# Attention by query blocks on quarters of the matmul array, with other stages' work placed between its steps

## The reference, cut to what matters

```python
h_c = modulate(rms_norm(ctx, g_norm_mix[layer]), csh_m, csc_m)
kc, vc = jnp.split(h_c @ w_in_l[:, Q_W:V_END], 2, axis=-1)
h_x = modulate(rms_norm(x, g_norm_mix[layer]), sh_m, sc_m)
qx, kx, vx, fx, glx = split_in_proj(h_x @ w_in_l)
qx = apply_rope(rms_norm(to_heads(qx, N_HEADS), g_q[layer]), cos, sin)
kx = apply_rope(rms_norm(to_heads(kx, N_KV_HEADS), g_k[layer]), cos, sin)
attn_x = blocked_attention(qx, k_all, v_all)   # softmax over 256 context + 2048 latent keys
g_attn, g_four = jnp.split(jax.nn.sigmoid(gate_logits + b_gate), N_BRANCH, axis=-1)
merged = g_attn * (attn @ w_attn_proj) + g_four * (fourier_mix(four) @ w_fourier_proj)
x = x + gt_m * (merged @ w_o)
x = x + gt_f * swiglu(modulate(rms_norm(x, g_norm_ffn[layer]), sh_f, sc_f), w_gate_up[layer], w_down[layer])
return rms_norm(x, g_final)
```

## Time and profile before

| | us |
|---|---|
| median of 3 runs | 1676.18 (1675.09 to 1676.6) |
| profiled execution, device time | 1671.44 |
| its span, slowest core | 1670.1 |
| PE busy, share | 1439.7, 86% |
| ACT busy, share | 925.3, 55% |
| DVE busy, share | 741.0, 44% |
| spans of the eight cores | 1653.5 to 1670.1 |

### The profile page before, as it was taken

How to read it: one execution, slowest core, us unless ns; L and a number is a source line. 1 busy time by engine, 2 the same in 40 slices (tenths; PEclk the granted TensorE clock), 3 DMA queues, 4 the chain that set the end, 5 groups by cost and what they waited for, 6 DMA issues and landing times.

```text
span 1670.1 us, 24822 instructions; the slowest of 8 cores (1653.5 to 1670.1 us)
## 1 busy us (share of the span) xinstructions
PE 1439.7 (86%) x7012; PEld 551.1 (33%) x7012; DVE 741.0 (44%) x994; ACT 925.3 (55%) x1470; POOL 36.4 (2%) x51
## 2 busy tenths in 40 slices
PE   0476668999999999999989999457899999999997
PEld 0232233222222222222334444213344444444443
DVE  3177779646555555555553333124311111212344
ACT  2587773999999999999922222017921111112111
POOL 1000000000000000000010000100000000000000
PEclk9999999999999999999999999679999999999999
DMA  9911100000000000000471130795682122202232
GB/s 191 158 38 39 51 14 1 1 1 1 14 1 1 14 1 1 14 1 1 54 98 22 24 45 1 142 168 182 173 168 48 29 40 37 51 26 76 107 116 81
DMA packets 48551, 93.16 MB, mean 56 GB/s; under 512 B 3233, under 2 KB 34082, under 8 KB 46754
## 3 DMA queue, kind: packets, MB, share of 16 engines
q0 software_dynamic: 34160, 43.52, 17.6%
q1 hardware_dynamic: 14258, 48.06, 8.6%
HBM read 118.31 MB, written 16.78 MB: 81 GB/s over the span
## 4 chain that ended last, share of the span: by engine, by line
PE 73%; DVE 8%; DMA 6%; ACT 6%; issue 5%; DVEq 0%; POOL 0%; ACTq 0%; POOLq 0%; another core or an unknown queue 0%
PE PS L353 73%; DMA SB<-w_ada 6%; ACT SB L377 6%; DVE SB L381 5%; DVE SB L411 2%; DMA SB<-w_in 1%; DVE SB L420 1%; PE PS L357 0%; DVE SB L405 0%; DVEq L254 0%; ACT SB L410 0%; POOL SB L262 0%; ACTq L254 0%; ACT L377 0%
## 5 line engine op out<-in xcount | busy, mean ns | idle before, releaser
L353 PE MATMUL PS<-SB 128*128 128x512 bf16 (+4 forms) x6540 | 1411.4, 375 | 171.7 <-DMA SB<-w_ada 67.5
L353 PEld LDWEIGHTS PS<-SB 128*128 128x128 bf16 (+1 forms) x6540 | 520.7, 98 | 1038.8 <-issue 614.6
L377 ACT ACTIVATE SB<-PS 128x1024 bf16<-128x1024 f32 (+2 forms) x714 | 607.3, 1003 | 258.3 <-PE PS L353 255.9
L381 DVE TENSOR_TENSOR SB<-PS,SB 128x512 f32<-128x512 f32 (+4 forms) x290 | 184.4, 664 | 579.6 <-PE PS L353 545.3
L377 ACT ACTIVATE SB<-SB 128x8 f32<-128x8 f32 (+3 forms) x285 | 145.8, 512 | 222.4 <-DVE SB L381 196.6
L381 DVE TENSOR_TENSOR SB<-SB 128x128 bf16<-128x128 f32 (+8 forms) x464 | 237.7, 531 | 46.9 <-DMA SB<-x 11.2
L377 ACT ACTIVATE SB<-PS,SB 128x128 bf16<-128x128 bf16 (+1 forms) x336 | 145.9, 531 | 184.8 <-PE PS L353 141.7
L417 DVE RECIPROCAL SB<-SB 64x512 f32<-64x512 f32 x64 | 214.2, 3347 | 4.2
L411 DVE COPY SB<-PS 128x1024 f32<-128x1024 f32 (+1 forms) x40 | 44.5, 1116 | 225.0 <-PE PS L353 224.8
L357 PE MATMUL PS<-SB 128*128 128x128 bf16 x472 | 40.7, 230 | 49.2 <-ACT SB L377 29.8
L410 ACT COPY SB<-PS 128x512 bf16<-128x512 bf16 (+2 forms) x50 | 35.5, 720 | 47.7 <-PE PS L353 23.7
(11 more groups left out here) (10 smaller groups left out, 11.7 us busy)
## 6 DMA issues: line engine op xcount, KB each, us to landing
SB<-x SPq DMA_DIRECT2D x32, 512.0 KB, 4.5
SB<-w_ada POOLq DMA_DIRECT2D x12, 1024.0 KB, 19.9
SB<-w_gu POOLq DMA_DIRECT2D x11, 1024.0 KB, 8.7
x_scratch<-SB SPq DMA_DIRECT2D x16, 512.0 KB, 5.3
SB<-x_scratch SPq DMA_DIRECT2D x16, 512.0 KB, 3.4
out<-SB SPq DMA_DIRECT2D x16, 512.0 KB, 2.6
SB<-w_dn POOLq DMA_DIRECT2D x2, 2816.0 KB, 32.6
SB<-w_in POOLq DMA_DIRECT2D x4, 1024.0 KB, 60.6
```

Of the source, the lines that this page charges most:

```text
L353: return K.op("pe", lambda h: h.matmul(out.ap, lhsT=lhsT.ap, rhs=rhs.ap, start=start, stop=stop), reads=[lhsT, rhs], writes=[out], cost=12 ...
L377: return K.op("act", lambda h: h.activation(out=out.ap, in_=in_.ap, func=func, **kw), reads=reads, writes=writes, cost=ecost("act", in_))
L381: return K.op(eng, lambda h: h.tensor_tensor(out=out.ap, in0=a.ap, in1=b.ap, op=op), reads=[a, b], writes=[out], cost=(1600.0 if op == ALU ...
```

## The change

The change rewrites the plan and the layout of nearly all stages.

- All weights are packed on the host so that each partition's part is contiguous (w_ada in 12 pieces of 16 KB a partition, w_in split into w_q, w_kv, w_f, and w_mix, which joins the gate, attention and Fourier projection columns of two column blocks). The columns of w_q and the rows of w_ap are permuted by heads.
- Phase A makes keys and values for 18 tiles (context last) and queries for the first block of 512 tokens alone. `P1` copies the transposed tile out of PSUM unmodulated in one ACT copy; `MOD` modulates two tiles at a time on DVE in place, bf16, eight tensor_scalar operations. The key is not doubled any more, and keys of two heads lie on the two halves of the partitions.
- Attention runs query block by query block (4 blocks, 8 units each). Key-query and value products each use four matmuls with 64x64 weights, one on each quarter of the array. The softmax sum is formed from bf16 additions of the probability tiles on DVE (13 additions of 128x1024 a unit) and then ten 512-column matmuls with a ones matrix; at the end of a unit DVE adds the two halves of the numerator and takes reciprocals in four pieces of 128. Scores have two pairs of banks; six buffers hold the probabilities; banks 6 and 7 are for other work.
- Between the steps, queries of the next block, the Fourier projection, its DFTs, the late modulation, and the merge groups of the first token block are placed, metered by a credit of 1.6 atoms a step (an atom is about one 512-column matmul). Gates use Tanh of half the argument in place of Sigmoid, with the factor one half put into the gate GTm.
- After attention, the merge of token blocks 1 to 3 (and what is left of block 0), with w_o and the first tiles of x loaded during it. In E1 the modulation is on DVE and the reciprocal root is two POOL operations, as in the final norm.
- The planner goes by the recorded order, with three lower classes of priority for filler matmuls, has a price for changing between the full and the quartered array, and latencies by engine.

```diff
+    LAT = {"pe": 390.0, "act": 190.0, "dve": 190.0, "pool": 300.0, "sp": 100.0}
+    LOW = 1 << 20
+    MIX = 1 << 21
+    LAST = 1 << 22
+    SWITCH_NS = 105.0
+    AHEAD_NS = 130.0
...
-                    heapq.heappush(rh, (-nd.bl, i, nd))
+                    heapq.heappush(rh, (nd.prio, i, nd))
...
+            if e == "pe":
+                top = run_h[e][0][2] if from_run else wait_h[e][0][2]
+                if top.prio >= self.LOW:
+                    soon = [it for it in wait_h[e][:40] if it[2].prio < self.LOW and it[0] <= st + self.AHEAD_NS]
+                    if soon:
+                        it = min(soon)
+                        wait_h[e].remove(it)
+                        heapq.heapify(wait_h[e])
+                        st, _, n = it
...
+            if e == "pe" and n.mode != pe_mode:
+                pe_mode = n.mode
+                st += self.SWITCH_NS
...
-    wada_d = din("w_ada", [D, 6 * D])
+    wada_d = din("w_ada", [12, 128, 4096])
...
+    wmix_d = din("w_mix", [4, 128, 7168])
...
+    ada_seq = ((1, 0), (1, 1), (0, 0), (0, 1))
+    for i in range(4):
+        ada_load(ada_slots[i], (0, 1)[ada_seq[i][0]], ada_seq[i][1])
+    loadw(Wkv, wkv_d.rearrange("p (k n) -> p k n", k=8))
+    for i in range(4):
...
+    def rstd(dst, ms, n=1):
+        ts("pool", dst, ms, EPS, ALU.add)
+        tt("pool", dst, dst, sub(mhalf, mhalf.ap[:, 0:n]), ALU.pow)
...
+        cp("act", dst, sub(pT, pT.ap.rearrange("p (k t) -> p k t", k=8)), outs=outs)
+
+    def MOD(t):
+        for k in range(8):
+            if t < NT:
+                o = (t // 4) * 4096 + k * 512 + (t % 4) * 128
+                v = rng(hT, hT.ap[:, t // 4, k, (t % 4) * 128:(t % 4) * 128 + 256], o, o + 256, 2)
+                m = 0
+            else:
+                v = rng(hcT, hcT.ap[:, k, :], k * 256, k * 256 + 256, 2)
+                m = 2
+            ts("dve", v, v, rng(modc, modc.ap[:, m, k:k + 1], m * 8 + k, m * 8 + k + 1, 4), ALU.mult,
+               rng(modc, modc.ap[:, m + 1, k:k + 1], m * 8 + 8 + k, m * 8 + 9 + k, 4), ALU.add, per=0.27)
+
...
+        act(sq, pv, AF.Square, scale=0.125)
+        tt("dve", h3(u), h3(pv), sub(tabv, tab(0).unsqueeze(1).to_broadcast([128, nh, 64])), ALU.mult)
+        tt("dve", h3(w), h3(pv), sub(tabv, tab(1).unsqueeze(1).to_broadcast([128, nh, 64])), ALU.mult)
+        reduce_sum(ss, h3(sq))
+        rstd_act(rs, ss, nh)
+        tt("dve", h4(u), h4(u), swapped(w, nh), ALU.add)
+        tt("dve", h3(outb), h3(u), sub(rs, rs.ap.unsqueeze(2).to_broadcast([128, nh, 64])), ALU.mult)
...
+    def Q_groups(qb):
+        for hf in range(2):
+            for tl in range(4):
+                if qb == 2:
+                    add_group(1, 10, late_ada.pop(0), 286)
+                    add_group(1, 0, ada_prefetch, 286)
+                add_group(max(qb - 1, 0), 9, lambda t=qb * 4 + tl, hf=hf: Qhalf(t, hf), 144 * qb - 2)
+
+    late_ada = [lambda vi=vi, hf=hf: ada_late_cols(vi, hf) for vi in (2, 3) for hf in range(2)]
+    late_ada += [lambda gt=gt, v=v, hf=hf: ada_late_rows(gt, v, hf) for gt, v in ((GTm, 2), (GTf, 5)) for hf in range(2)]
+    N0, N1 = 144 + 16, 432
+    add_group(0, 0, load_f, N0)
+    Q_groups(1)
+    for fg in range(4):
         for tb in range(4):
...
-            act(gsl[0], pGa, AF.Sigmoid, bias=sub(bgate, bgate.ap[:, j:j + 1]))
...
+    def give(qb, n):
+        credit[0] += n
+        while groups and credit[0] > 0 and groups[0][0] <= qb:
+            emit_group()
+        credit[0] = min(credit[0], 4.0)
...
+    def qk(n):
+        qb, c, kt = steps[n]
+        p = c // 4
+        b0 = (n % 2) * 2
+        parts = []
+        for kc in range(2):
+            for h in range(2):
+                o = p * NKT * 128 + kt * 128 + kc * 64
+                l_ = rng(kT, kT.ap[h * 64:(h + 1) * 64, p, kt * 128 + kc * 64:kt * 128 + kc * 64 + 64], o, o + 64, 2)
+                r_ = rng(qT, qT.ap[h * 64:(h + 1) * 64, qb, c, :], qb * 4096 + c * 512, qb * 4096 + c * 512 + 512, 2)
+                lo = (b0 + h) * 2048
+                o_ = View(PS[kc * 64:kc * 64 + 64, (b0 + h) * 512:(b0 + h + 1) * 512], "ps", lo, lo + 2048)
+                parts.append((o_, l_, r_, True, True))
+        mms(parts, mode=1, cost=216.0)
+
+    def av(n):
+        qb, c, kt = steps[n]
+        pt = PTs[n % NPT]
+        p = c // 4
+        parts = []
+        for r in range(2):
+            for h in range(2):
+                hd = 2 * p + h
+                l_ = rng(V, V.ap[r * 64:(r + 1) * 64, kt, hd * 64:hd * 64 + 64], kt * 256, kt * 256 + 256, 2)
+                parts.append((half(4 + r, h), l_, sub(pt, pt.ap[r * 64:(r + 1) * 64, h * 512:(h + 1) * 512]),
+                              kt == 0, kt == NKT - 1))
+        mms(parts, mode=1, cost=216.0)
+
...
+            tt("dve", slot, a, b, ALU.add, per=0.52)
+        else:
+            slot = cur["sums"][-1]
+            tt("dve", ptmp, a, b, ALU.add, per=0.52)
+            tt("dve", slot, slot, ptmp, ALU.add, per=0.52)
...
+        cp("dve", xs, bank(4), late=-30)
+        tt("dve", xs, xs, bank(5), ALU.add, late=-30)
+        ss = cur["sums"]
+        b = next_bank()
+        K.level = 1
+        for i, s_ in enumerate(ss):
+            for h in range(2):
+                mm(bank(b), sub(ones, ones.ap[:, h, :]), sub(s_, s_.ap[:, h * 512:(h + 1) * 512]),
+                   i == 0 and h == 0, i == len(ss) - 1 and h == 1)
+        K.level = 0
+        cp("dve", rd, bank(b))
+        at = attnTs[qb]
+        L = 60
+        for hh in range(4):
+            v = rng(rd, rd.ap[:, hh * 128:(hh + 1) * 128], hh * 128, hh * 128 + 128, 4)
+            recip(v, v, late=L)
+        tt("dve", rng(at, at.ap[:, c, :], c * 512, c * 512 + 512, 2), xs, rd, ALU.mult, late=L)
+        credit[0] -= 10
...
+    def step(n):
+        qb, c, kt = steps[n]
+        pt = PTs[n % NPT]
+        act(pt, s_bank(n), AF.Exp)
+        if n + 2 < len(steps):
+            qk(n + 2)
+        if kt % 2 == 1:
+            av(n - 1)
+            av(n)
+            pair_add(n)
...
+    RATE = 1.6
+    for t in range(4):
+        P1(t)
+    MOD(0)
+    MOD(2)
+    for t in range(4):
+        KV(t)
+        Qhalf(t, 0)
+    for t in range(4, NKT, 2):
+        P1(t)
+        P1(t + 1)
+        MOD(t)
+        KV(t)
+        KV(t + 1)
+    for t in range(4):
+        Qhalf(t, 1)
+    qk(0)
+    qk(1)
+    bank_set[0] = [6, 7]
+    for n in range(len(steps)):
+        qb, c, kt = steps[n]
+        drain(n)
+        step(n)
+        if kt == NKT - 1:
+            finish_unit(qb, c)
+        give(qb, RATE)
+    K.level = 3
...
+            act(tF if part else tA, bank(b), AF.Tanh, scale=0.5, bias=rng(bgate, bgate.ap[:, jb:jb + 1], jb, jb + 1, 4))
+        elif part == 1:
+            group(b, 8, lhs, lambda k: at_v(tb, k))
+            stt("dve", tA, tA, 1.0, bank(b), ALU.add, ALU.mult)
+        else:
```

More of the change, by code:

```diff
@@ L53, in __init__ @@
         self.tk = None
-        self.bl = 0.0
+        self.prio = 0
+        self.mode = 0
 class _Rec:
@@ new lines, in mms, with fn @@
+    def mms(parts, mode=0, cost=None):
+        def fn(h):
+            for o_, l_, r_, st_, sp_ in parts:
+                ins = h.matmul(o_.ap, lhsT=l_.ap, rhs=r_.ap, start=st_, stop=sp_)
+            return ins
+        if cost is None:
+            cost = sum(max(30.0, 2.0 + 0.418 * fsz(p[2])) for p in parts)
+        reads, seen = [], set()
+        for p in parts:
+            for v in (p[1], p[2]):
+                if (v.sp, v.lo, v.hi) not in seen:
+                    seen.add((v.sp, v.lo, v.hi))
+                    reads.append(v)
+        writes, seen = [], set()
+        for p in parts:
+            if (p[0].lo, p[0].hi) not in seen:
+                seen.add((p[0].lo, p[0].hi))
+                writes.append(p[0])
+        return K.op("pe", fn, reads=reads, writes=writes, cost=cost, mode=mode)
@@ new lines, in half, with group, trs, fn @@
+    def half(b, h):
+        lo = b * 2048
+        return View(PS[h * 64:(h + 1) * 64, b * 512:(b + 1) * 512], "ps", lo, lo + 2048)
+    def group(b, nk, lhs, rhs, more=False):
+        for k in range(nk):
+            mm(bank(b), lhs(k), rhs(k), k == 0, k == nk - 1 and not more)
+    def trs(pairs, ident):
+        def fn(h):
+            for o_, i_ in pairs:
+                ins = h.transpose(out=o_.ap, in_=i_.ap, identity=ident.ap)
+            return ins
+        return K.op("pe", fn, reads=[p[1] for p in pairs] + [ident], writes=[p[0] for p in pairs], cost=64.0 * len(pairs))
@@ L362, in act @@
+    def act(out, in_, func, scale=1.0, bias=None, accum=None, late=0):
+        reads = flat([in_])
         kw = {}
@@ L481, in build @@
     load(gcols, gcols_d)
+    load(ident, ident_d)
     load(gq_bc, gq_d.partition_broadcast(128))
```

1075 lines of the change are left out of this document (528 added, 547 removed).

## The result

The changed kernel takes 1595.35 us (median; 1594.25 to 1596.59), 0.952 of the time before, interval 0.950 to 0.954. It is 81 us faster; the prediction said 176, and 1595 is above its range too. The direction was right and the size was not.

A forecast was written before the change was run, and what follows sets the result against it. Outside attention, merge and feed-forward PE was half idle; that work moves into attention, bound by DVE. 1670.1 - 7.5 - 125.4 + 108.4 - 32.8 - 31.6 - 88.3 = 1492.9, 1500 us to be measured, range 1440 to 1590.

The forecast's parts named there:

- DVE's sum: Attention: all DVE work adds to 623 us, 1.08 a step, so DVE becomes the bound, just over PE and ACT.
- land at about 43 instead of 50, and four tiles are normalised meanwhile: Start-up: early w_ada pieces land sooner beside x and the key table; modc at 47.5 instead of 55, -7.5 us.
- I add 4% to the highest: Attention: four limits between 1.0 and 1.08 a step and a fixed order give 1.12 a step, 645 us.
- Rival 2: Attention: the two-bank chain and wrong planner costs make 1.3 a step, 749 us, total 1604; chance 0.13.
- The chain of two banks: Attention: Exp n, key-query group n+2, Exp n+2 take 0.87 us a step, or 1.03 with one filler and mode change.
- 144 steps x 1.6 - 8 x 10 = 150 atoms: Attention and merge: block 0 merge matmuls fitting into attention by credit, 32 us, leaving (896 - 150) x 0.216 = 161 us.
- the w_gu and w_down loads stand behind those roots: E1, POOL's queue: these loads follow the roots but have a whole pair's time in hand; no cost counted.
- the price of the modulation: E1: eight small DVE operations at 0.12 us a tile, within DVE's 3.7; the stage taken at 4.4 a tile, 70 us.
- rivals 3 and 4: Attention: column halves run serially, total 1707 us, chance 0.04; or bf16 additions take 1.22 us, total 1749, chance 0.02.
- The warning that queued fillers could hold the freeing of the sums: Attention: a sign that would prove the prediction wrong, queued fillers delaying the freeing of the sums; no size given.
- The changes of array mode: Attention, PE: two or three changes between full and quartered array a step at 0.10 us, 115 to 170 us.
- the second way of rival 3: Attention: quarters' weight loads stand before each group, 0.4 us a group, 1.79 a step, total above 1850; chance 0.02.

The follow-up runs named there:

- ada_split4: Each w_ada piece loaded by four instructions with 2 KB packets instead of 8 KB, against the changed kernel: 1582.57 us, ratio 0.946 to the kernel before.
- half_adds: Eight of the 13 softmax-sum additions of each unit left out, against the changed kernel: 1594.76 us in one execution.
- rate185: Filler credit of 1.85 atoms a step in place of 1.6, against the changed kernel: 1591.84 us, 0.9505 of the kernel before.
- one_wait: Only the last wait of each semaphore kept instead of one for each predecessor, against the changed kernel: 1573.35 us, 0.940 of the kernel before.
- e1_mod_act: Two of eight E1 modulations a tile moved from DVE to ACT, against the changed kernel with single waits, split w_ada loads and look-ahead off: 1529.37 us, for 1532.48.

## Why the prediction was wrong, point by point

In the attention the mechanism failed: it was put at DVE's sum and 4%, and that sum doesn't bind. In the start-up and in E1 a wait was put at nothing (x beside large packets, 15 us; the roots behind queued waits, 18 us), and in the merge a term was too small by 17. The four misses make 112 us; the span is over by 102, as two stages came out 10 below.

- **Start-up (+23.6).** The step that failed is "land at about 43 instead of 50, and four tiles are normalised meanwhile". It priced the pieces by w_gu's 8.7 us alone on its queue and gave x nothing for the company. x landed at 50, and PE's fixed order put the pieces' matmuls behind x's transposes. 15 us of it are shown to be the packets, by ada_split4; for the remaining 8, PE waits for w_ada again, until 53.95 and not 43.
- **Phase A (-4.1).** 112 was near: 107.9, with DVE and ACT 70% busy rather than 80.
- **Attention (+32).** Each price was right (a group of four at 0.22, the addition 0.66, Exp and reciprocal as before), and so was ACT: 591 predicted, 587 busy, though partly by luck, since the Exps cover 547 where 527 stood and the rest 40 for 64. PE's 610 lies in its 570 to 625. DVE's sum was 54 too high, 569 for 623. The step that failed is "I add 4% to the highest" of four limits. The highest was no limit: half_adds took 156 us off DVE and gained 3. The nearest bound is ACT's sum, at 587 to 597: a bare unit has ACT busy 98%, though no run took work off ACT to show it. The distance from it is placement: 15% in the changed kernel, 7% without the look-ahead. Rival 2 had the mechanism ("wrong planner costs", a fixed order) with too high a price, 749. The chain of two banks doesn't hold bare units, which run at 17.1 us, 0.95 a step; with a filler in its way it was priced at 1.03, and no run tests that alone.
- **Merge (+21).** "144 steps x 1.6 - 8 x 10 = 150 atoms" began block 3 with a credit of zero. Groups that are forced out when due are charged all the same, so credit is deep below zero there, and the gates show what came in: 5, not 11. A gate stands for 14 matmuls, so 896 - 5 x 14 = 826 are left for the merge, not 746: 80 x 0.216 = 17. The rest of the 21 is the boundary, behind which the first matmuls of E1 already run. This is no loss by itself: rate185 shows that what the merge sheds the attention takes.
- **E1 (+35).** 17.6 are the queued waits, shown by one_wait. The prediction looked at this queue and went by in the wrong order: it saw "the w_gu and w_down loads stand behind those roots", where some of the roots stand behind the loads, and the loads behind 174 and 173 waits. Some 0.9 us a tile, up to 14, is the price of the modulation (0.23 for 0.12); e1_mod_act shows that at most a part of that counts. What is left of the 35 beyond the waits, 17 (22 from where the merge ends), is otherwise open.
- **Feed-forward (-5.4)**: not changed, as predicted, but for the place of the boundary.
- **What held**: the quarters (rivals 3 and 4 are out), phase A, that late modulation and the Fourier stage vanish from the open, PE full in the merge (184.00 of 184.00), no wait for w_ada outside the start-up. The warning that queued fillers could hold the freeing of the sums looked at the fillers, but the larger loss, 36 us, was the order in which the look-ahead put them, for which the prediction had nothing but its 4%. The changes of array mode as such are within its 115 to 170: 1032, or 1.8 a step, at 0.14 and 0.09.
- The Trainium skill ("TensorEngine Tiling (Array Packing)", "Restrictions and Gotchas") says that column tiling excludes the Fast Weight Load; the prediction weighed it as the second way of rival 3. Whether or not the quarters' weight loads are slower for it (0.106 each, where the full ones take 0.099), the next group of four starts some 0.22 behind the last, and of 194.49 us of loads in the 677 at least 127 lie beside matmuls, since PE is idle for 67.0. The measurement decides against it as a cost in this kernel.

## What to carry to other kernels

When work is moved under a stage that has room, sum the engines, but then look at the order: ask at which step each piece falls due, whether pieces come in runs, and what a scheduler's rule does to the order, in pauses so short that the profile counts them as busy. An idle stretch costs twice when the clock falls behind it. Read each queue that a moved transfer passes instruction by instruction, its waits included: long fulfilled waits are not free, and what stands behind them pays. When an edit that should remove a wait gains nothing, look in its trace whether the wait is gone: here it was, and a new cost had taken its place. Size a transfer's packets by its neighbours, too: large packets on one queue can starve another with small ones.

## What the runs showed of the hardware that was not expected

- Packet size decided how two queues shared the DMA engines. With w_ada in 8 KB packets x took 45.2 us to land, with 2 KB packets 16.6, at the same bytes; a 32 KB load 24.4 and 8.4.
- A fulfilled wait cost POOL some 61 ns: 174 of them held a load for over 10 us.
- Four quarter matmuls of 512 columns cost one full matmul, 0.22, and their four 64-column weight loads of 0.10 lie beside matmuls at no cost. From a full matmul to a group of quarters it is 0.31 to 0.36, and back 0.31.
- Behind 4.37 us of idle PE the granted clock was 0.54 over the next eight matmuls, 0.43 us each in place of 0.216.
- A 128x128 bf16 modulation with two per-partition operands keeps DVE 0.23 us and ACT 0.44 us.
